# A 31-tap convolution summed in PSUM by pairs of tiles, and a linear recurrence whose levels are spread over the projections around them

## The reference, cut to what matters

```python
proj = h @ w_in
(cv_a, cv_g, hg_q, hg_f, hg_i, hg_g, sb_q, sb_k, sb_v, gl) = split(proj)
# convolution branch: 512 channels, 31 taps, causal, one filter a channel
u = cv_a * sigmoid(cv_g)
u = conv(u, conv_w) + conv_b
y_conv = silu(layer_norm(u)) @ w_conv_proj
# recurrence: 4 heads of 128 x 128, decay 1 - k
k = (1 - lb) * sigmoid(-hg_f)
state = (1 - k) * state + k^T v        # token by token
y_hgrn = (rms_norm(silu(hg_q) @ state) * silu(hg_g)) @ w_hgrn_proj
# stick-breaking attention from rms-normed sb_q, sb_k, and sb_v
merged = gate0 * y_conv + gate1 * y_hgrn + gate2 * y_sb
```

## Time and profile before

| | |
|---|---|
| median of 3 runs | 3629.01 us (3629.0 to 3630.0) |
| the profiled execution | 3628.38 us, span 3626.6 us |
| TensorE (PE) busy | 3473.3 us, 96%, 15544 matmuls |
| VectorE (DVE) busy | 1635.0 us, 45% |
| ScalarE (ACT) busy | 1291.5 us, 36% |
| GpSimd (POOL) busy | 1797.6 us, 50% |

### The profile page before, as it was taken

One profiled execution on the slowest core, in us unless ns is written; L12 is line 12 of the kernel. 1 busy time (PEld: TensorE's weight loads), 2 busy tenths in 40 slices (PEclk: granted clock), 3 DMA queues, 4 the chain that ended last, 5 costly groups with the idle time before them and its releaser, 6 DMA issues.

```text
span 3626.6 us, 46811 instructions
## 1 busy us (share of the span) xinstructions
PE 3473.3 (96%) x15544; PEld 2800.9 (77%) x15544; DVE 1635.0 (45%) x2482; ACT 1291.5 (36%) x1760; POOL 1797.6 (50%) x2327
## 2 busy tenths in 40 slices
PE   5968899999999999999999999999999999999999
PEld 4846666678888888778878888888887788788887
DVE  4955655544445433750333334453348313243433
ACT  3333344432223222662553222232226635532221
POOL 4732222355555555555335555555555543365554
PEclk8989999999999999999999999999999999999999
DMA  5211134322222222222122322222222221222222
GB/s 193 93 52 41 47 122 139 110 100 98 94 97 93 98 98 93 87 76 99 59 71 94 110 93 98 98 93 98 93 98 82 87 87 65 70 93 99 94 97 104
DMA packets 90983, 336.95 MB, mean 93 GB/s; under 512 B 10096, under 2 KB 10480, under 8 KB 90224
## 3 DMA queue, kind: packets, MB, share of 16 engines
q1 hardware_dynamic: 85392, 313.68, 24.9%
q10 hardware_dynamic: 5472, 21.65, 1.8%
HBM read 333.19 MB, written 2.10 MB: 92 GB/s over the span
## 4 chain that ended last, share of the span: by engine, by line
PE 85%; DVE 6%; DVEq 3%; ACT 3%; issue 2%; POOL 0%; ACTq 0%; POOLq 0%
PE ps L429 25%; PE ps L431 25%; PE ps L430 25%; DVE arena L1624 1%; PE ps L670 1%; DVEq L1622 1%; PE ps L514 1%; PE ps L812 1%; PE ps L558 1%; PE ps L559 1%; PE ps L560 1%; PE ps L792 1%; DVE arena L1930 1%; PE ps L684 1%; PE ps L685 1%
## 5 line engine op out<-in xcount | busy, mean ns | idle before, releaser
L420 POOL TENSOR_TENSOR w_lo<-raw,w_hi 128x256 fp32r<-128x256 f32 x2280 | 1787.3, 816 | 1807.6 <-ACT w_hi L893 1807.4
L893 ACT ACTIVATE w_hi<-raw 128x1024 fp32r<-128x1024 f32 x572 | 602.0, 1055 | 1069.5 <-PE ps L431 1042.4
L429 PE MATMUL ps<-a_hi,w_lo 128*128 128x512 f32 x2256 | 900.8, 399 | 34.6 <-POOL w_lo L420 21.7
L431 PE MATMUL ps<-a_hi,w_hi 128*128 128x512 f32 x2256 | 881.9, 391 | 0.0
L430 PE MATMUL ps<-a_lo,w_hi 128*128 128x512 f32 x2256 | 881.2, 391 | 0.0
L429 PE MATMUL ps<-b_hi,w_lo 128*128 128x512 f32 x2112 | 827.3, 392 | 4.2 <-DVE b_lo L1563 4.0
L431 PE MATMUL ps<-b_hi,w_hi 128*128 128x512 f32 x2112 | 822.8, 390 | 0.0
L430 PE MATMUL ps<-b_lo,w_hi 128*128 128x512 f32 x2112 | 822.7, 390 | 0.0
L429 PEld LDWEIGHTS ps<-a_hi,w_lo 128*128 128x128 f32 x2256 | 425.8, 189 | 132.3 <-POOL w_lo L420 23.0
L430 PEld LDWEIGHTS ps<-a_lo,w_hi 128*128 128x128 f32 x2256 | 425.9, 189 | 90.0 <-issue 4.5
L431 PEld LDWEIGHTS ps<-a_hi,w_hi 128*128 128x128 f32 x2256 | 425.1, 188 | 90.5
(11 more groups left out here) (236 smaller groups left out, 2713.7 us busy)
## 6 DMA issues: line engine op xcount, KB each, us to landing
raw<-in_stream SPq DMA_DIRECT2D x573, 512.0 KB, 3.2
arena<-in_mod_w ACTq DMA_DIRECT2D x32, 512.0 KB, 4.1
arena<-in_mod_w SPq DMA_DIRECT2D x16, 512.0 KB, 8.0
xres<-in_x_t SPq DMA_DIRECT2D x1, 2048.0 KB, 7.7
xres<-in_x_t ACTq DMA_DIRECT2D x1, 2048.0 KB, 7.5
arena<-in_lru ACTq DMA_DIRECT2D x2, 1024.0 KB, 6.9
out_t<-xres SPq DMA_DIRECT2D x1, 2048.0 KB, 6.3
arena<-in_c_row SPq DMA_DIRECT2D x1, 512.0 KB, 9.1
```

Source lines behind the costliest of these rows:

```text
L420: last = pool.tensor_tensor(w_lo[:, s, part], raw[:, s, part], w_hi[:, s, part].bitcast(F32), ALU.subtract)
L429: pe.matmul(out, lo, x_hi, start=start, stop=False)
L431: return pe.matmul(out, hi, x_hi, start=False, stop=stop)
L893: act.activation(w_hi[:, slot, :], raw[:, slot, :], ACT.Copy).then_inc(hi_ready, 1)
```

## The change

**Buffers.** `conv_out` moves from `arena`, where the recurrence's sums, exponents and products lie, to the upper half of `xres` (the residual, which is read last by the first norm and loaded anew later).

**Convolution.** The four input tiles get four banks (2 to 5) in place of two. VectorE convolves tiles 0 and 1 when these two are there, then 2 and 3. First tap and taps 1 to 29 write a sum in PSUM (banks 2 and 3), the last tap writes `conv_out`. The sum over channels is asked for one unit earlier, before the last g unit.

**Recurrence.** Head 0 runs beside the values, q, k and gates that come ahead of the convolution's projection. Each later head's levels stand one by one at the middles and ends of units. The output of head h-1 comes in the middle of the half projection of round h, its norm later. VectorE asks for the next head's logarithm before the last two merges. Each gate pair is evacuated raw and put through one Sigmoid of 128 x 1024 in SBUF, after the pair. The stream order puts q and k units ahead of the gates.

```diff
-        conv_in, conv_out = area(U0, CT, PAD + S), area(C0, CT, S)
+        conv_in, conv_out = area(U0, CT, PAD + S), xres[:, CT:2 * CT, :]
...
+            c.dve.ring = WIDE
             project_fresh(bank_v(), bank_a())
             for j in range(1, CT):
                 project(bank_v())
                 project(bank_a())
+            c.dve.ring = 2
             for h in range(2 * HG_HEADS):
                 project(bank_a())
+            pe.wait_ge(dve_evacuated, c.dve.at(0))
             values_4(0)
             for h in range(HG_HEADS):
                 project(bank_a())
+                if h == 2:
+                    conv_mean()
...
+            def beside_values(t):
+                hgrn_level(0, t)
+                if t == 1:
+                    stats(CT)
+            def stats_level(h, n, weights=ones_p):
+                stats(1, weights)
+                hgrn_level(h, n)
+            def beside_conv(h, m):
+                if m == 0:
+                    hgrn_out(h - 1)
+                hgrn_level(h, m)
+            def norm_level(h):
+                stats(1)
+                c.op.n += 1
+                hgrn_level(h, 2)
+            values_2(beside_values)
+            c.op.n += CT
+            project(bank_a(), lambda: hgrn_level(0, 4))
+            hgrn_level(0, 5)
+            project(bank_a(), lambda: stats_level(0, 6, pair_ones[:, :]))
+            hgrn_level(0, 7)
+            project(bank_a(), lambda: stats_level(0, 8, pair_ones[:, :]))
+            hgrn_level(0, 9)
             project(bank_a())
+            for h in range(1, HG_HEADS):
+                pe.wait_ge(op_ready, c.op.at(0))
+                project_half(0, lambda m: beside_conv(h, m))
+                project(bank_a(), lambda: norm_level(h))
+                hgrn_level(h, 3)
+                project(bank_a(), lambda: stats_level(h, 4, pair_ones[:, :]))
+                hgrn_level(h, 5)
+                project(bank_a(), lambda: stats_level(h, 6, pair_ones[:, :]))
+                hgrn_level(h, 7)
+                project(bank_a(), lambda: hgrn_level(h, 8))
+                hgrn_level(h, 9)
+            project_half(0, lambda m: hgrn_out(HG_HEADS - 1) if m == 0 else None)
+            values_2(lambda t: stats(1) if t == 0 else None)
...
+            def gate_in(m):
+                need(act, dve_evacuated, c.dve.at(0))
+                evacuate(sgate[:, m % 2, :], ACT.Identity, bias=par(PAR1, "gate_b", m))
+            def gate_pair():
+                act.drain()
+                act.activation(sgate[:, :, :], sgate[:, :, :], ACT.Sigmoid).then_inc(sigmoid_ready, 1)
+            hgrn_log()
+            tick()
+            evacuate(hg_g[:, HG_HEADS - 1, :], ACT.Silu)
+            logs()
+            tick()
+            hgrn_decays(0, 1)
...
+            for h in range(1, HG_HEADS):
+                hgrn_log()
+                tick()
+                pass_v(2)
+                hgrn_decays(0, 1)
+                act.wait_ge(head_done, h)
+                square(ps[:, 6, :])
+                hgrn_decays(2)
+                tick()
+                hgrn_decays(3)
+                inverse_rms(P)
+                hgrn_decays(4)
+                sb_operand(sb_q[:, h, :])
+                round_tiles(b_hi, [4 + h - 1])
+                tick()
+                hgrn_decays(5)
+                inverse_rms(SB_DH)
+                hgrn_decays(6)
+                sb_operand(sb_k[:, h, :])
+                tick()
+                hgrn_decays(7)
+                inverse_rms(SB_DH)
+                gate_in(2 * h)
+                tick()
+                hgrn_decays(8)
+                gate_in(2 * h + 1)
+                gate_pair()
...
+            def conv_pair(first):
+                both = [(j, ps[:, 2 + j % 2, :]) for j in (first, first + 1)]
+                dve.drain()
+                for j, acc in both:
+                    dve.tensor_scalar(acc, conv_in[:, j, 0:S], params[:, taps + j:taps + j + 1], par(PAR1, "conv_b", j), ALU.mult, ALU.add)
+                with dve.Fori(1, TAPS - 1) as tap:
+                    dve.drain()
+                    for j, acc in both:
+                        dve.scalar_tensor_tensor(acc, conv_in[:, j, bass.ds(tap, S)], params[:, bass.ds(tap * CT + (taps + j), 1)], acc,
+                                                 ALU.mult, ALU.add)
...
+            c.dve.ring = WIDE
+            conv_input(0)
+            conv_input(1)
+            conv_pair(0)
+            conv_input(2)
+            conv_input(3)
+            c.dve.ring = 2
+            conv_pair(2)
...
+            for h in range(1, HG_HEADS):
+                head = following
+                head.levels(0, 2)
+                gated_conv(h - 1)
+                pass_a(4)
+                head.levels(2, 5)
+                hgrn_norm(h - 1)
+                head.levels(5, 7)
+                hgrn_low(h - 1)
+                sb_normalise(sb_q[:, h, :], q_col)
+                head.levels(7, 9)
+                sb_normalise(sb_k[:, h, :], par(PAR1, "sbk_g"))
+                if h < HG_HEADS - 1:
+                    following = Head(h + 1)
+                    following.keys()
+                head.last_merges()
+                if h < HG_HEADS - 1:
+                    following.sums()
...
+    order += list(moving(cut(4096, 256))) + sb_qk[0:2] + list(gate[0:2])
     for h in range(1, HG_HEADS):
+        order += [conv_proj[h - 1]] + sb_qk[2 * h:2 * h + 2] + list(gate[2 * h:2 * h + 2])
+    order += [conv_proj[3]] + list(moving(cut(4352, 256)))
```

More of the change, by code:

```diff
@@ L479, in project_fresh, with project_half @@
                     tile(made)
-            def project_half(first):
+            def project_half(first, after=None):
                 s = unit()
@@ L568, in _, with conv_mean @@
             x_stats()
+            def conv_mean():
+                pe.wait_ge(aux_evacuated, c.aux.at(0))
+                pe.wait_ge(conv_ready, c.conv.at(1))
+                c.conv.n += 1
+                for j in range(CT):
+                    last = pe.matmul(ps[:, 6, :], ones_p, conv_out[:, j, :], start=j == 0, stop=j == CT - 1)
+                last.then_inc(mean_done, 1)
+            c.dve.ring = WIDE
             project_fresh(bank_v(), bank_a())
@@ L639, in _ @@
[L639 to L658, removed]
-                    after = ((0, 1), (2, 3, 4), (5, 6), (7, 8, 9))
-                    values_2(lambda t: hgrn_levels(h, *after[t]))
-                hgrn_out(h)
@@ L1005, in _ @@
             values_4(hg_v)
-            for h in range(HG_HEADS):
+            for h in range(HG_HEADS - 1):
                 tick()
@@ L1043, in _ @@
+            logs()
+            tick()
+            hgrn_decays(0, 1)
+            for j in range(2):
+                act.wait_ge(centred, j + 1)
+                square(conv_out[:, j, :])
+            hgrn_decays(2)
+            sb_value(0, 0)
+            for j in range(2, CT):
+                act.wait_ge(centred, j + 1)
+                square(conv_out[:, j, :])
+            hgrn_decays(3)
+            inverse_rms(CONV_CH)
+            hgrn_decays(4)
             sb_value(0, 1)
             tick()
-            gates(PAR1, "gate_b", 0)
@@ L1095, in _ @@
+            square(ps[:, 6, :])
+            tick()
             inverse_rms(P)
             round_tiles(b_hi, [7])
+            sb_value(1, 0)
+            sb_value(1, 1)
+            tick()
             def load_late(u):
@@ L1608, in _, with conv_input @@
             norm(a_hi, a_lo, scale1, modp[:, 0:KT])
-            for j in range(CT):
+            taps = PAR1["conv_w"][0]
+            def conv_input(j):
                 a = v_tile()
@@ new lines, in _ @@
+            head.levels(0, 4)
+            dve.wait_ge(rt_ready, c.rt.at(1))
+            c.rt.n += 1
+            for j in range(CT):
+                last = dve.tensor_tensor(conv_out[:, j, :], conv_out[:, j, :], rt, ALU.mult)
+            last.then_inc(normalised, 1)
+            head.levels(4, 8)
+            sb_normalise(sb_q[:, 0, :], q_col)
+            head.levels(8, 9)
+            sb_normalise(sb_k[:, 0, :], par(PAR1, "sbk_g"))
+            following = Head(1)
+            following.keys()
```

224 lines of the change are left out of this document (87 added, 137 removed).

## The result

The changed kernel takes 3570.61 us (median of four runs, 3568.57 to 3572.43) against 3629.01 before: ratio 0.9838, with a 95% interval of 0.9821 to 0.9855, so 58.4 us faster. The forecast of 3577 is 6.4 us too high; the result lies in its range and in the likeliest case's own (3564 to 3592), though nearer to the figure of the second rival, 3567.

The account below looks back on a forecast made before the run. TensorE bounds the kernel, losing 90 us to waits and slow clock. 174.3 + 204 work + 27 waits + 9 clock + 2 = 416.3 against 468.6 before: gain 52.3, median 3577 us; 8 in 10 for 3560 to 3603.

Parts of the forecast that it names:

- the likeliest case: Whole kernel: the forecast of 3577 us, chance 0.70, range 3564 to 3592, its upper end allowing convolution rounds of 1.8 us.
- the second rival: Recurrence: level tails overlap, no collisions, clock stays up at two boundaries; 3567 us, chance 0.13.
- The convolution: VectorE's taps: 1.50 us a round, end at 166.7, 7.6 us before the sum over channels is wanted, so no wait.
- Rival 1: Convolution: stays slow in PSUM, 2.20 us a round, end at 210.1, wait 35.8; 3611 us, chance 0.12.
- The rule that I left out: VectorE's access costs about 60 ns on SBUF, 125 on PSUM: convolution end near 179, wait 5 us, sum 3582.
- Head 0: TensorE waits 2.8 us at the first level, 3.0 at level 8, 2.8 at the operand of the convolution's projection.
- The head boundary: First level of heads 1 to 3: 4.4 + 7.5 - 5.8 = 6.1 us wait, three times, 18 us.
- my lower bound of 5.0: Wait per head boundary at least 5.0 us, with output 2.1 us longer covered and no collision.
- Within a head: Heads 1 to 3: level waits cost nothing, level 8 with thin cover of 0.4 us; head period 48 to 50.
- TensorE's own work: TensorE's busy time at full clock, from the third g unit to the stick-breaking stage: 204 us.
- collisions and handoffs: Recurrence: 4 us, less 2 for level tails counted twice, so 2 in the sum.
- Clock: TensorE at low clock after first-level waits, 2.2 us lost on average; three boundaries and one more: 9 us.

Follow-up runs that it names:

- the constant tap: Changed kernel with a constant in place of the params column as scalar in the loop of 29 taps, values left out: 3569.27 us, one run.
- e7_keys_late: Changed kernel with the scaling of the keys and the request for the logarithm put behind the last two merges, as before: 3569.98 us.
- e1_conv_only: Kernel before with the new convolution alone (four banks, pairs, sums in PSUM), recurrence as before: 3601.11 us.
- e3_old_conv: Changed kernel with the convolution of before (all four inputs first, four tiles a round, sums in SBUF): 3604.45 us.
- e4_inputs_first: Changed kernel with pairs in PSUM, but both pairs convolved after all four inputs: 3590.61 us.
- e8_all: `e6_sums_early` with head 0's exponentials, Silu, copies and low parts earlier, and its level 8 in the middle of the second gate unit: 3539.35 us.
- e6_sums_early: Changed kernel with ScalarE's logarithm before the gate tile, VectorE's running sums before the last merge, two Exps before the weight rounding: 3548.69 us.
- the two kernels run once: Changed kernel, loop of 29 taps with a constant scalar, or with a column at a fixed address: 3569.27 and 3562.91 us.

## Why the prediction was right, and where its terms were off

**The convolution: the right mechanism, one term too small.** The sum took 0.60 + 0.70 + 0.20 = 1.50 us a round; it is 1.61 and 1.69. The rows behind 0.60 and 0.70 (L1635, L1837 and L1533 in the earlier trace rows) have no column among their inputs; the taps do. The costliest groups on the page of the changed kernel's profile have the same line without and with one:

```profile
L1922 DVE SCALAR_TENSOR_TENSOR xres<-ps,xres 128x512 f32<-128x512 f32 x368 | 246.8, 689 | 180.4 <-PE ps L431 170.2
...
L1922 DVE SCALAR_TENSOR_TENSOR xres<-ps,cols,xres 128x512 f32<-128x512 f32 x136 | 99.2, 749 | 73.4 <-PE ps L431 70.9
```

The second group stood on the page of before as well, with 748 ns, and the prediction did not use it. 60 ns, twice a round, are 0.12 x 62 = 7 us; the gap of the second pair is 2.5 more; a start 0.7 us earlier took a little back. The end came at 175.1 in place of 166.7, the 7.6 us to spare were used up, and 1.9 us of wait came out where I had none. The range had room for it (rounds of 1.8). Rival 1, the contended pace in PSUM, did not come: no round is longer than 1.42 beside GpSimd's work.

The rule that I left out says about 60 ns of access on SBUF and about 125 on PSUM for a VectorE instruction (the Trainium skill, Perfetto Trace Analysis, section Optimizing Scalar/DVE Operations). By it the pair in SBUF should take 0.13 less than in PSUM; measured, both take 1.41 us when GpSimd is idle. The 0.62 and 0.69 that I had set against the rule settle nothing, though: the first row has no column among its inputs and the second has one, and that alone is worth 0.06. Its estimated end of the convolution, near 179, was nearer to 175.1 than mine, but for a reason that the constant tap shows to be another one.

**Head 0** was right: waits of 2.15, 2.79 and 2.90 us against 2.8, 3.0 and 2.8.

**The head boundary** was right in mechanism and in its three pieces: evacuation to logarithm 4.4 (4.4 forecast), logarithm to product 7.0 (7.5), TensorE's cover 5.8 (5.8). The waits are 3.70, 5.70 and 5.70, together 15.1 against 18.3. At the two later ones 0.4 is missing: I had added 0.5 for a meeting with GpSimd that the 7.0 of the earlier trace rows already held; one shows (0.94 us at 298.20 for a subtraction that the same line makes in 0.41 at 299.40). At the first one 2.4 is missing, for a reason that the prediction did not have: TensorE's cover is 7.8 us there, because level 9 comes a unit earlier and in its place stand the rest of the operand's wait and the slow clock behind it. In the execution of `e7_keys_late`, where the clock stayed at 1.00 behind that wait, it is 5.11. That 3.70 even lies below my lower bound of 5.0, and the bound was ill worked out: the two things named for it, 2.1 us more cover and no collision, would have given 3.5. That pulling the scale and complement ahead is worth nothing, as the sum took it, was right too.

**Within a head** no level waits, level 8 neither, as forecast with 0.4 us of cover. The head period is 48.5 and 49.7 us (first-level starts 252.12, 300.65, 350.39), in the 48 to 50.

**TensorE's own work was the largest error**: 204 us, plus 2 for collisions and handoffs. The stage shows 210.04 - 9.3 = 200.7, and the kernel without low clock 200.9. The same working on the other runs places the 3 us. With the old order of the recurrence it gives 204.3 (before) and 203.2 (`e1_conv_only`, 50.4 us idle); with the new order 200.6 (`e3_old_conv`, 59.5 us idle), 200.8 (`e4_inputs_first`) and 200.9 (`e8_all`, 5.2 us idle). So it comes with the new order and not with the idle time. The old order has over twenty separate waits in the stage and the new one some seven; that the tails and first matmuls around each are what costs is a guess, no run isolates it. Collisions cost nothing within a head, as no level of heads 1 to 3 waits there; this is the part of the second rival that came true.

**Clock**: 9 us forecast, 9.3 measured. That they meet so closely is luck: `e7_keys_late`, whose time is the same, lost 11.0 in its profiled execution. The fall that opened the stick-breaking stage is gone, as forecast.

The errors add up: work and collisions 206 to 200.7 (-5.3), waits 27 to 24.4 (-2.6), clock +0.3, together the 7.6 by which the stage starts earlier (408.7 against 416.3). The medians differ by 6.4, as the profiled execution lay 2.0 below its median and the one of before 0.6.

## What to carry to other kernels

When two waits stand in a row on the engine that bounds, price them together: the new order of the recurrence was worth 25 us with the old convolution and 31 with the new one, and the new convolution needed both its bank and its early start. Where a wait is left at a stage boundary, follow the queue of the engine that makes its first operand: here one logarithm moved ahead of a gate tile and two table loads on ScalarE brought 20 us, while asking for it earlier on VectorE brought nothing. Take durations only from rows with the same operands, the scalar's included.

## What was not expected of the hardware

- A scalar read from a column costs VectorE 60 ns over none on 128x512 float32 (0.705 against 0.645 us in the chain of taps; 749 against 689 ns in two groups on the page of the profile).
- The gap between rounds of a loop on VectorE depends on the addresses in it: 0.20 and 0.28 us for the same code at two places with a column from the loop's register, 0.15 and 0.17 with a fixed one, 0.08 with the loop written out. Why the two places differ is open.
- A tile in SBUF beside a sum in PSUM is not slowed by GpSimd at all (1.41 us a pair of taps); with both in SBUF a pair takes up to 2.1 beside it, and GpSimd's own instructions take 1.11 us in place of 0.69.
- The granted clock does not follow the waits alone: the 2.79 us wait was followed by 0.50 in `e6_sums_early` and by 1.00 in the changed kernel, and of the two kernels run once, one had 8 us more at the low level. What part of the 20 us from 10.7 us of shorter waits another kernel would see is open.
